# Two down projections whose pairs of output tiles are computed in turn between two PSUM banks

## The reference

```python
def sq_relu_mlp(h, w_up, w_down):          # h: 256 x 1024
    return jnp.square(jax.nn.relu(h @ w_up)) @ w_down
...
        x = x + sq_relu_mlp(rms_norm(x, norm_ffn_g[layer]), ffn_w_up[layer], ffn_w_down[layer])
```

## Time and profile before

| what | value |
|---|---|
| median of 3 runs | 1201.04 us (1201.02 to 1203.13) |
| profiled execution, first to last instruction | 1203.7 us |
| TensorE busy, share of the span | 98% |
| VectorE, ScalarE, GpSimd busy | 73%, 54%, 25% |
| D0, first to last matmul | 227.4 to 317.6 us |
| D1, last matmul | 592.8 us |
| mean granted TensorE clock | 0.994 |

### The profile page before, as it was taken

One profiled execution on the slowest core, in us unless ns is written; L12 is line 12 of the kernel. 1 busy time (PEld: TensorE's weight loads), 2 busy tenths in 40 slices (PEclk: granted clock), 3 DMA queues, 4 the chain that ended last, 5 costly groups with the idle time before them and its releaser, 6 DMA issues.

```text
span 1203.7 us, 26180 instructions
## 1 busy us (share of the span) xinstructions
PE 1180.3 (98%) x9666; PEld 1155.8 (96%) x9666; DVE 875.4 (73%) x1383; ACT 644.8 (54%) x1055; POOL 295.9 (25%) x285
## 2 busy tenths in 40 slices
PE   7999999999999999999999999999999999999997
PEld 6998999999997999999999999999999999999997
DVE  7776766656696766756667578888767678888853
ACT  4666555544446555543445456666544455665533
POOL 4001400012230500023400263344321025444421
PEclk9999999999999999999989999999999999999999
DMA  9643555555652655464544345554556555555461
GB/s 295 193 140 97 184 181 182 195 175 174 158 167 71 184 193 183 163 202 161 172 142 142 106 140 176 177 190 161 170 191 210 194 176 176 175 188 186 134 201 58
DMA packets 212097, 203.52 MB, mean 169 GB/s; under 512 B 11824, under 2 KB 211760, under 8 KB 212032
## 3 DMA queue, kind: packets, MB, share of 16 engines
q1 hardware_dynamic: 211888, 202.44, 52.6%
q10 hardware_dynamic: 144, 0.20, 0.1%
HBM read 201.57 MB, written 1.05 MB: 168 GB/s over the span
## 4 chain that ended last, share of the span: by engine, by line
PE 94%; DVE 3%; issue 1%; ACT 1%; POOL 1%; DMA 0%; DVEq 0%; POOLq 0%; ACTq 0%
PE gemm L719 28%; PE gemm L721 28%; PE gemm L720 28%; PE gemm L730 2%; PE gemm L731 1%; PE gemm L732 1%; DVE w_lo L1599 1%; PE score L910 1%; DVE act_a L1608 1%; PE score L1025 1%; PE misc L755 0%; DMA w_raw<-in_fox_w_in 0%; PE score L1028 0%; PE score L1128 0%; PE gemm L927 0%
## 5 line engine op out<-in xcount | busy, mean ns | idle before, releaser
L1599 DVE TENSOR_TENSOR w_lo<-w_raw,w_hi 128x1024 fp32r<-128x1024 f32 (+2 forms) x404 | 483.5, 1201 | 158.5 <-ACT w_hi L1238 157.1
L719 PE MATMUL gemm<-act_a,w_hi 128*128 128x256 f32 x1704 | 489.0, 287 | 9.3 <-DVE act_a L1608 8.8
L1238 ACT CAST w_hi<-w_raw 128x1024 fp32r<-128x1024 f32 (+2 forms) x404 | 401.3, 998 | 173.7 <-PE gemm L721 168.2
L720 PE MATMUL gemm<-act_a,w_hi 128*128 128x256 f32 x1704 | 484.6, 284 | 0.0
L721 PE MATMUL gemm<-act_a,w_lo 128*128 128x256 f32 x1704 | 484.4, 284 | 0.0
L719 PEld LDWEIGHTS gemm<-act_a,w_hi 128*128 128x128 f32 x1704 | 329.3, 193 | 14.0 <-DVE w_lo L1599 9.4
L720 PEld LDWEIGHTS gemm<-act_a,w_hi 128*128 128x128 f32 x1704 | 329.7, 193 | 0.1
L721 PEld LDWEIGHTS gemm<-act_a,w_lo 128*128 128x128 f32 x1704 | 329.5, 193 | 0.0
L719 PE MATMUL gemm<-hid,w_hi 128*128 128x256 f32 x864 | 242.1, 280 | 0.0
L720 PE MATMUL gemm<-hid,w_hi 128*128 128x256 f32 x864 | 241.7, 280 | 0.0
L721 PE MATMUL gemm<-hid,w_lo 128*128 128x256 f32 x864 | 241.7, 280 | 0.0
(11 more groups left out here) (268 smaller groups left out, 1406.7 us busy)
## 6 DMA issues: line engine op xcount, KB each, us to landing
w_raw<-in_ffn_w_up SPq DMA_DIRECT2D x76, 1024.0 KB, 5.2
w_raw<-in_ffn_w_down SPq DMA_DIRECT2D x32, 1024.0 KB, 4.9
w_raw<-in_gla_w_in SPq DMA_DIRECT2D x12, 1024.0 KB, 5.3
w_raw<-in_ffn_w_down SPq DMA_DIRECT2D x16, 768.0 KB, 4.1
w_raw<-in_sc_w_in SPq DMA_DIRECT2D x12, 1024.0 KB, 5.1
w_raw<-in_fox_w_in SPq DMA_DIRECT2D x11, 1024.0 KB, 5.8
w_raw<-in_ffn_w_down SPq DMA_DIRECT2D x16, 640.0 KB, 3.8
w_raw<-in_fox_w_out SPq DMA_DIRECT2D x4, 1024.0 KB, 4.9
```

The lines of the kernel that those rows point to most:

```text
L719: nc.tensor.matmul(ps, wh[:, k, cols], act[:, k0 + k, 0, :], start=start and k == 0, stop=False)
L720: nc.tensor.matmul(ps, wh[:, k, cols], act[:, k0 + k, 1, :], start=False, stop=False)
L1238: nc.scalar.copy(split_half(w_hi, nc_, nj), raw_half(nc_, nj)).then_inc(w_hi_ready, 1)
L1599: nc.vector.tensor_tensor(split_half(w_lo, nc_, nj), raw_half(nc_, nj), split_half(w_hi, nc_, nj).bitcast(F32), ALU.subtract).then_inc(w_l ...
```

## The change

In `down` on TensorE the two halves of a chunk are no longer computed one after the other. A new function, `paired_blocks`, goes through the eight input tiles of a chunk once; for each it issues six matmuls that alternate between the two banks: high by high for tile 0 and tile 1, high by low for both, low by high for both. Before a chunk it waits for both split halves, and before cc = 0 for both banks. `half_done` is raised by each bank's last matmul, so by two at the end of the pair. Nothing changes on the other engines.

```diff
+            def paired_blocks(banks, c, act, k0, start, stop, tiles):
+
+                wh = [split_half(w_hi, c, j) for j in range(2)]
+                wl = [split_half(w_lo, c, j) for j in range(2)]
+                nk = kind_of(c)[1]
+                last = [None, None]
+                for k in range(nk):
+                    pe.wait_ge(act_ready, tiles + k + 1)
+                    for j in range(2):
+                        nc.tensor.matmul(banks[j], wh[j][:, k, :], act[:, k0 + k, 0, :], start=start and k == 0, stop=False)
+                    for j in range(2):
+                        nc.tensor.matmul(banks[j], wh[j][:, k, :], act[:, k0 + k, 1, :], start=False, stop=False)
+                    for j in range(2):
+                        last[j] = nc.tensor.matmul(banks[j], wl[j][:, k, :], act[:, k0 + k, 0, :], start=False,
+                                                   stop=stop and k == nk - 1)
+                for j in range(2):
+                    last[j].then_inc(half_done, 1)
...
                     for cc in range(4):
                         c = C0[stage] + cc
-                        for j in range(2):
-                            b = (b0 + j) % 4
-                            split_ready(c, j, it)
-                            if cc == 0:
-                                pe.wait_ge(*before[b])
-                                pe.wait_ge(dve_evac, DE[stage] + j - 1 + 2 * i)
-                            feature_block(gemm[b][:, 0:T], c, j, hid, k0=8 * cc,
-                                          start=cc == 0, stop=cc == 3,
-                                          tiles=tiles + 8 * cc if j == 0 else None).then_inc(half_done, 1)
+                        split_ready(c, 1, it)
+                        if cc == 0:
+                            for j in range(2):
+                                pe.wait_ge(*before[(b0 + j) % 4])
+                            pe.wait_ge(dve_evac, DE[stage] + 2 * i)
+                        paired_blocks([gemm[(b0 + j) % 4][:, 0:T] for j in range(2)], c, hid, 8 * cc, cc == 0, cc == 3,
+                                      tiles + 8 * cc)
```

## The result

The changed kernel takes 1234.55 us (median of 4 runs, 1233.15 to 1236.4) against 1202.09 us for the kernel before in the same comparison: 1.0263 times the time (95% interval 1.0240 to 1.0286), 32.5 us more. The forecast was 1231 us. The profiled execution of the changed kernel spans 1231.2 us, that of the kernel before 1203.7.

The account below looks back on a forecast made before the run. The prediction took TensorE, busy for 98% of the span, and its matmul pace as the bound. Bank stalls 17.4, stage ends 2.1 and 2.7, and clock falls 7.7 sum to 29.9 us on 1201.04: 1231 us, range 1219 to 1240.

Parts of the forecast that it names:

- Nothing to remove: Down stages: no stall left before the matmuls of L719, L720 and L721; only their pace, 117.3 ns each, remains.
- a repeated bank does not set the pace: Down-stage matmuls: a bank change comes 0.11 us apart like its neighbours, so alternating 1536 matmuls is worth 0.
- the lower bound: Down-stage matmul pace: transposes 0.11 us apart, about 110 ns, would mean 11 us gained over 1536 matmuls.
- The banks at a turn's end: Behind three turns of each down stage TensorE waits for both banks' multiplies: 6 x 2.90 = 17.4 us.
- The ends: After D0 the last x tile's multiply comes 2.1 us later; after D1 GpSimd's chain of sums starts 2.7 us later.
- The weights: Inside a turn, splitting of weight halves stays hidden, 1.8 us to spare; tightest at the stage's start, by 0.3 us.
- The clock: Behind the new stalls TensorE's clock falls for 3.4 us, 1.54 us each: 7.7 us, bounds 0 and 18.4 us.
- Five of six stalls: At the turns' ends in both down stages, 5 clock falls were taken for 6 stalls: 7.7 us.
- Holding of the clock: Rival: at the new stalls the clock holds or falls once or twice; loss 22.2 to 25 us, about 1224; chance 0.15.
- the long falls: Rival: clock stays down 6.8 us at most stalls, or pace goes to 120 ns; about 1238; chance 0.11.
- The quicker pace: Rival: alternation quickens the down stages' matmuls to about 110 ns; 19 us lost, about 1220; chance 0.05.
- the other side: Rival: kernel not slower, as down-stage matmuls below 102.8 ns pay for the stalls; 1197 us at 100 ns; chance 0.02.

Follow-up runs that it names:

- e5: e4 with both multiplies first on VectorE and the next turn's weight halves split ahead of the residual's rounding on ScalarE and VectorE; 1208.38 us, ratio 1.0038.
- e1: The changed kernel with VectorE's order at a turn's end altered: both multiplies first, then the additions, the weight subtraction last; 1218.83 us, ratio 1.0128.
- e2: The changed kernel with its waits and signals kept, but bank 1's 24 matmuls after bank 0's 24 instead of alternating; 1235.64 us, ratio 1.0254.
- e7: The changed kernel with the fourth turn of each down stage computed half after half as before; 1221.55 us, ratio 1.0143.
- e4: The changed kernel with two pairs of banks, for odd and even turns, VectorE's and ScalarE's order kept; 1218.7 us, ratio 1.0118.
- e6: The kernel before, without alternation, with the two statistics blocks behind D1 issued one half of GQK later; 1200.94 us, ratio 0.9973.

## Why the prediction came out right

**Nothing to remove.** The reading of rows 2 to 4 holds. e5 measures the step "a repeated bank does not set the pace" by itself: 0.00 us over D0. (The transposes that I took as the lower bound move 128 columns and not 256, so they say little of these matmuls.) The 109.2 ns that I had worked out from the Trainium skill's formula ("TensorE: Matmul & The Clock Gate", "Back-to-back issue gap") are not reached by alternating banks: e5 keeps the kernel's 117.3 ns, so whatever makes the difference is not the bank.

**The banks at a turn's end.** Forecast 2.90 us for each stall, with the second multiply at 252.45 and the restart at 252.92. The trace has 252.37 and 252.84; in the after trace everything before lies about 0.06 us earlier. A stall is 2.89 us from start to start, less the 0.12 of a normal step, plus 0.11 for the late second matmul: 2.88, so 17.3 us for six against 17.4. e1 shows that the order on VectorE makes it (1.01 where the subtraction moves away), e2 that the waits alone suffice, and e7 that half a chunk of offset was the cover.

**The ends.** D0: the last wait moved the next stage by 1.98 us against 2.1. (The next stage's starts lie 12.1 us later than in the kernel before at D0's end, and 14.1 where KVQ's second half begins.) The term was right in size but not in the tile: TensorE first stands for tile 6, whose low part is made behind the second multiply too, from 331.87 to 334.07. D1: the statistics matmul is at 633.00 against 601.43, 31.57 us later, and D1's last matmul 28.84 later: 2.73 against 2.7. TensorE at D0's end, then GpSimd's chain behind D1 and TensorE's wait for it:

```profile
331.87 0.28 PE L721 MATMUL gemm<-act_b,w_lo 128*128 128x256 f32 x1
334.07 0.38 PE L719 MATMUL gemm<-act_b,w_hi 128*128 128x256 f32 x1 [1.91 <-DVE act_b L1624]
...
623.07 1.52 POOL L672 TENSOR_TENSOR sqt<-x 128x256 f32 x1 [18.81 <-DVE x L1700]
...
632.23 0.72 POOL L679 TENSOR_TENSOR ssq<-ssq,sqt 128x256 f32<-128x256 f32 x1
...
631.25 0.28 PE L721 MATMUL gemm<-act_a,w_lo 128*128 128x256 f32 x1
633.00 0.70 PE L773 MATMUL misc<-ssq,con 128*128 128x256 f32 x2 [1.48 <-POOL ssq L679]
```

**The weights.** The half ready at 232.95 by the forecast was ready at 231.69 + 1.23 = 232.92. The subtraction forecast to end near 257.5 ended at 257.46:

```profile
231.69 1.23 DVE L1615 TENSOR_TENSOR w_lo<-w_raw,w_hi 128x1024 fp32r<-128x1024 f32 x1 [0.22 <-DVE rstd L1651]
...
256.25 1.21 DVE L1615 TENSOR_TENSOR w_lo<-w_raw,w_hi 128x1024 fp32r<-128x1024 f32 x1
```

No pair waits for weights. e4 adds what the forecast did not say: this holds only because the stall itself gives the time. Take the stall away and 1.9 and 1.1 us of it come back at the next pair.

**The clock.** This term was undersized. The price of a fall was right (1.54 us in D1's turns). "Five of six stalls" came out too, but it was a guess: e2 has six of six, e7 three of four. I counted falls only behind the turns. The ends of the stages are idle time too, and each had a fall, at 336.17 and 626.30. The one behind D0 is new and cost 1.5 us: D1 starts 15.58 us later than before, and KVQ's second half had started 14.10 later. The one behind D1 cost nothing: it ended at 629.71, and TensorE, slower or not, then still waited for GpSimd's chain until 633.00. So six falls count, 9.1 us and not 7.7.

**The sum.** The two traces can be compared part by part up to the statistics matmul behind D1. Six stalls are 17.3 us, five falls inside the stages 7.6, D0's end 2.0 and the fall behind it 1.5, D1's end 2.7, and a slower pace in D0 0.5: 31.6 us, where the trace has 31.57 and the forecast had 29.9. What the forecast left out is the fall behind D0 and that pace.

Behind this matmul the difference shrinks again. The profiled execution of the kernel before (by its span the run of 1205.58 us, the slowest of its first four) had a fall of 6.8 us there and one of 3.4 us at 693.98; the changed kernel's has neither, and by 876.69 its delay is down to 26.99 us. These two falls of the kernel before cost 4.6 us. So the two spans differ by 27.5 us only, and the medians, 32.5 us apart, depend on how many such falls the runs of the kernel before had: against its median of 22 runs, 1204.8, the changed kernel's 1234.55 is 29.7 us more. That the total came within 4 us of the forecast is well founded; that it came nearer than some 2 us, by either median, is luck. In the 22 runs the kernel before took 1200.9 us where the mean granted clock was 0.998 and 1205.8 where it was 0.994. I took the distance between the profile's span and the median (2.7 us) as fixed; it is the clock of that execution. It still led to a fair start: the profiled run of 1205.58 us less its 4.6 us of falls is 1201.0.

The slower pace in D0 is not one of alternation. There the second and the fourth turn run at 118.7 ns a matmul outside a fall, the third at 117.3, like all of D1. e2, which does not alternate, has the same: 118.7, 117.3 and 118.7 in the turns behind D0's three stalls; and e7's fourth turns, computed half by half, run at 118.7. Turns with no stall ahead of them were at 117.3 in every run. So a stream that starts again after a stall runs at the one pace or the other for a whole turn, worth 0.25 us; what decides it these runs don't show.

**The rivals.** Holding of the clock (0.15) and the long falls (0.11) lay to either side of what came. Long falls did not occur at the turns; e2 and e1 had one of 6.8 us each behind D1. The quicker pace and the other side are ruled out by e5. On the mechanism that the Trainium skill describes on the same page ("A second HAM failure mode: psum-queue depth-cycling"): cycling through banks itself opened no gap here (e5, four banks and no idle time), the waits for their draining did, and those brought the falls.

## What to carry to other kernels

Two output tiles that are computed one after the other hide each other's way out of PSUM; computed in turn they finish together, and the next tiles wait for both unless there are banks for them. When both ends of a pair move together, look at the reader's own order: here most of the stall (1.9 of 2.9 us, by e1) was work that the reader did between the two reads without need, and behind that wait stood the next one, for weights. And look at each new wait of TensorE of 2 us or more for a fall of its clock behind it, at the ends of stages as well as in the loops; the fall costs time of its own unless TensorE must wait for another engine right behind it anyway. Last, count the falls that the kernel before has already, for a profile of one execution has them in its span.

## What the runs showed of the hardware

- Alternating fp32r matmuls of 128 x 128 by 256 columns between two PSUM banks, with a weight change at each, run at 117.3 ns each, the same as into one bank (e5). After a stall of TensorE a whole turn can run at 118.7 ns instead, alternating (changed kernel, D0) or not (e2, e7).
- Gaps of 2.89 us from start to start, between full streams of matmuls, brought a fall to half clock in five of six cases in the changed kernel, gaps of 3.0 us in six of six in e2, and gaps of 2.89 us in three of four in e7. Gaps of 1.0 us (e1, six) and of 1.1 to 1.9 us (e4, six) brought none. Each fall inside the stages lasted 3.41 us and cost 1.5 us. A fall just ahead of a wait for another engine (changed kernel, 626.30) cost nothing.
- A 5 us spread between runs of an unchanged kernel (1200.9 to 1206.25) went with its mean granted clock (0.998 to 0.993). With the wait behind D1 filled (e6), 12 runs lay between 1199.46 and 1202.38.
